# Down projection: the fourth weight sum of each block is made by an accumulating DMA instead of VectorE

## The reference

```python
h = jnp.einsum('btd,df->btf', x, ffn_w_up)
h, new_ffn = causal_dwconv(ffn_hist, h, ffn_conv_w, ffn_conv_b)
hu, hg = jnp.split(h, 2, axis=-1)
f = jnp.einsum('btf,fd->btd', jax.nn.silu(hg) * hu, ffn_w_down)
x = layer_norm(ALPHA * x + f, ln2_g, ln2_b)
```

## Time and profile before

| | us |
|---|---|
| time, median of 3 runs (2047.17 to 2049.23) | 2048.83 |
| the profiled execution | 2046.75 |
| its span in the trace | 2044.9 |
| PE busy | 1992.1 (97%) |
| DVE busy | 1664.3 (81%) |
| ACT busy | 990.7 (48%) |
| POOL busy | 396.7 (19%) |

### The profile page before, as it was taken

One profiled execution on the slowest core, in us unless ns is written; L12 is line 12 of the kernel. 1 busy time (PEld: TensorE's weight loads), 2 busy tenths in 40 slices (PEclk: granted clock), 3 DMA queues, 4 the chain that ended last, 5 costly groups with the idle time before them and its releaser, 6 DMA issues. The chain is left out here.

```text
span 2044.9 us, 42398 instructions
## 1 busy us (share of the span) xinstructions
PE 1992.1 (97%) x15639; PEld 1972.5 (96%) x15639; DVE 1664.3 (81%) x2623; ACT 990.7 (48%) x1503; POOL 396.7 (19%) x552
## 2 busy tenths in 40 slices
PE   9999999999996999999999999999999999999995
PEld 8999999999996999999999999999999999999995
DVE  3698899987699877777777777777778889899898
ACT  4445444433565444444444444444446545454445
POOL 0022222120640211111111111111111121112212
PEclk9999999999997999999999999999999999999998
DMA  6322222123656766767667677676666898779973
GB/s 223 99 78 78 82 88 71 55 83 125 205 155 204 203 176 185 190 176 189 185 180 196 175 184 192 176 193 175 184 189 205 219 242 213 207 196 233 220 177 121
DMA packets 123246, 344.00 MB, mean 168 GB/s; under 512 B 14404, under 2 KB 24900, under 8 KB 123136
## 3 DMA queue, kind: packets, MB, share of 16 engines
q1 hardware_dynamic: 94336, 260.40, 38.0%
q0 software_dynamic: 27792, 80.19, 22.9%
q10 hardware_dynamic: 1008, 1.93, 0.3%
HBM read 314.04 MB, written 23.97 MB: 165 GB/s over the span
## 5 line engine op out<-in xcount | busy, mean ns | idle before, releaser
L1017 PE MATMUL acc<-comb,w_hi 128*128 128x274 f32 x4784 | 921.2, 292 | 17.6 <-DVE comb L2171 12.7
L1017 PEld LDWEIGHTS acc<-comb,w_hi 128*128 128x128 f32 x4784 | 759.6, 190 | 19.4 <-DVE comb L2171 7.4
L1017 PE MATMUL acc<-comb,w_lo 128*128 128x274 f32 x2392 | 693.0, 290 | 0.0
L1017 PEld LDWEIGHTS acc<-comb,w_lo 128*128 128x128 f32 x2392 | 458.0, 191 | 0.0
L1132 PE MATMUL acc<-comb,w_hi 128*128 128x272 f32 x2240 | 424.4, 288 | 3.6 <-DVE w_lo L2309 3.0
L1132 PEld LDWEIGHTS acc<-comb,w_hi 128*128 128x128 f32 x2240 | 352.3, 189 | 5.9 <-DVE w_lo L2309 3.6
L1132 PE MATMUL acc<-comb,w_lo 128*128 128x272 f32 x1120 | 323.3, 289 | 0.0
L1422 ACT ACTIVATE w_hi<-sum 128x1024 fp32r<-128x1024 f32 x172 | 182.4, 1060 | 239.9 <-PE acc L1017 137.2
L2119 DVE TENSOR_TENSOR w_lo<-sum,w_hi 128x1024 fp32r<-128x1024 f32 x172 | 210.8, 1226 | 81.0 <-ACT w_hi L1422 76.3
L2119 DVE TENSOR_TENSOR w_lo<-raw_a,w_hi 128x1024 fp32r<-128x1024 f32 x125 | 152.9, 1223 | 101.1 <-ACT w_hi L1422 101.1
L1132 PEld LDWEIGHTS acc<-comb,w_lo 128*128 128x128 f32 x1120 | 210.8, 188 | 0.0
(11 more groups left out here) (301 smaller groups left out, 3155.5 us busy)
## 6 DMA issues: line engine op xcount, KB each, us to landing
raw_a<-w_up SPq DMA_DIRECT2D x127, 512.0 KB, 6.1
stage<-w_stream SPq DMA_DIRECT2D x90, 512.0 KB, 3.3
sum<-w_up POOLq DMA_DIRECT2D x89, 512.0 KB, 7.0
sum<-w_up SPq DMA_DIRECT2D x88, 512.0 KB, 3.3
d_a<-w_down SPq DMA_DIRECT2D x96, 320.0 KB, 4.8
act_spill<-prod_f SPq DMA_DIRECT2D x43, 272.0 KB, 5.7
d_s<-w_down SPq DMA_DIRECT2D x32, 320.0 KB, 4.8
d_s<-w_down POOLq DMA_DIRECT2D x32, 320.0 KB, 6.5
```

The source lines that it names most:

```text
L1017: mm = pe.matmul(bank(b), wt[:, k * P:(k + 1) * P], prod_comb(j, k, c), start=start and q == 0, stop=stop and q == 2, skip_group_check=True)
```

## The change

The fourth sum is no longer an instruction of DVE. POOL issues an accumulating DMA (`sum_d_s4`) that adds quarter 1 of the block's weights, read again from HBM, to `d_s2`. It stands in POOL's stream after `add_x1` and before the sums of block b+2. It waits for the low part of product 2 (`up_lo`) and for its forerunner (`s4_first`, a semaphore that the up stage had used once, hence the 16). ACT's rounding for product 5 waits for its landing in place of `s4_made`. SP's load of `d_a12` of block b+1 no longer waits for the sum, only for the low part of product 1.

```diff
@@ SP
                 if b + 1 < N_BLOCKS:
-                    sp.wait_ge(s4_made, FT + b)
                     sp.wait_ge(up_lo, nth_down(b, 1))
                     load_d_a12(b + 1)
@@ ACT, down_top
                 elif s == 5:
-                    act.wait_ge(s4_made, FT + b)
+                    act.wait_ge(s4_first, 16 + 16 * (b + 1))
                     weight_top(n, d_s2[:, :])
@@ DVE
-            def make_d_s4(b):
-
-                dve.wait_ge(a12_in, 16 * (FT + b))
-                dve.wait_ge(up_lo, nth_down(b, 2))
-                dve.tensor_tensor(d_s2[:, :], d_s2[:, :], d_a12[:, :], ALU.add).then_inc(s4_made, 1)
...
                     low_after(b, s)
-                    if s == 1:
-                        make_d_s4(b)
@@ POOL
+            def sum_d_s4(b):
+
+                pool.wait_ge(up_lo, nth_down(b, 2))
+                pool.wait_ge(s4_first, 16 + 16 * b)
+                pool.dma_start(d_s2[:, :], dram["w_down"][b * 4 + 1], accum_op=ALU.add).then_inc(s4_first, 16)
...
                 if 1 <= b <= 8:
                     add_x1(b - 1)
+                sum_d_s4(b)
                 if b + 2 < N_BLOCKS:
                     sum_d_s1(b + 2)
```

## The result

| | before | after |
|---|---|---|
| median, us (lowest to highest) | 2048.84 (2047.17 to 2049.23), 4 runs | 2130.78 (2128.17 to 2131.39), 4 runs |
| ratio, with 95% interval | | 1.0406 (1.0394 to 1.0418) |
| profiled execution, its span | 2046.75, 2044.9 | 2130.52, 2128.9 |

The change costs 82 us. The direction was forecast, the size was not: 2081 was named, with a range up to 2112.

The account below looks back on a forecast made before the run. PE bounds the kernel, busy 97% of the span. Losses of 16.0, 14.4, 3.2 and 2 less 1 gained make 34.6 us, 32 after 3 off; 2046.75 becomes 2078.75, plus 2.08 to the median 2081, range 2062 to 2112.

Parts of the forecast that it names:

- the chain behind it: Before product 5: rounding 0.74, low part 0.73, add 0.44 and some 0.2 for hand-overs, 2.1 us together.
- a landing by 7.4: Block 13: the fourth sum must land by 7.4 us into the block, 1.4 after ACT's start in the kernel before.
- healing: Blocks 1 to 8: a stall before product 5 moves the next add_x1 and deadline back, so the 4.7 us loss partly shrinks.
- No healing: Rival, chance 0.11: each of 16 blocks loses its full 4.7 or 4.9 us, 77 us, with the rest 2130.
- the term 8 x 2.0 + 8 x 1.8: Loss of 2.0 us a block in blocks 1 to 8 (16.0) and 1.8 in blocks 18 to 25 (14.4).
- the round of the chain: Blocks 1 to 8: one d_s1 sum's issue to the next, 13.22 us, 15.2 with the new DMA, against a 13.2 block.
- the floors that I had for these two: Least landing of add_x1 with nothing in front (2.3 plus 3.3 us), and the new DMA's own work behind it, 1.96 us.
- my lower bound: Blocks 1 to 8: even with nothing ahead of add_x1, the new DMA lands 1.3 us after its deadline.
- the floor of 21 us: DMA engines at 94.8% plus 15% make 110%, so 16 blocks take at least 1.3 us more each, 21 us.
- the 3 us taken off: Deduction for SP's earlier d_a12 load, said to shorten the round a little: 34.6 becomes 32 us.

Follow-up runs that it names:

- The filler: Changed kernel plus 14 matmuls of ones (3.29 us) on PE ahead of product 5 in blocks 1 to 8 and 17 to 23: 2123.32 us, ratio 1.0377.
- The same traffic with the wait: Kernel before plus a 480-column accumulating DMA into an unused tile, whose landing ACT awaits before rounding for product 5: 2104.75 us, ratio 1.0273.

## Why the prediction was right and wrong

**Right: what is gained.** I took 1 us for VectorE's 26 us; leaving the sum out altogether gave 1.2, with an interval from 3.7 gained to 0.2 lost. The reading was that PE is busy 13.20 of 13.20 us and waits three times.

**Right: the place and the chain.** The waits are before product 5, ACT stands before the landing, and the chain behind it was worked out as 2.1 us and took 2.09. In block 6 product 5 could have started at about 1711.6, so ACT's latest start was 1709.5, 7.6 us into the block; I had a landing by 7.4. In the quiet blocks the DMA lands 4.7 us after issue in the median, mostly in time, and blocks 9 to 16 lost 2.2 us in all, with three waits of up to 0.5.

**Right: healing.** `add_x1` landed 6.5 us after issue where it took 9.1 before; in the run with the extra DMA, where nothing waits, it still takes 9.2 in the median, so it is the stalls that give the queue time. `add_shift` did not land sooner after its issue (11.6 us in the median where it was 10.3); what heals in blocks 18 to 25 is that it is issued 2.5 to 5.6 us before the block begins, where it was between 2.8 before and 0.9 behind. "No healing" named 2130 and the time is 2130.78, but its mechanism is refuted: the late part of the landing did shrink. That the number fits is chance, a smaller wait with a clock cost on top.

**Wrong: the term 8 x 2.0 + 8 x 1.8.** Measured idle time is 23.5 us in blocks 1 to 8 (2.9 a block) and 19.5 in blocks 18 to 25 (2.4 a block), with block 0 at 3.0 instead of 1.6. In the sum it is 51.8 against 34.6. The step that failed is "Between 1.3 and 4.7 I take the round of the chain", with its "With 1.96 more in this chain it is 15.2, against a block of 13.2: 2.0 us a block". That chain, from one `d_s1` sum to the next, doesn't close the loop: POOL stood idle in it for 9.11 us, waiting for a load. The loop that closes goes through PE: last product of a block, issue of `add_x1`, its landing, the fourth sum's landing, rounding and low part, product 5, product 6, and so again the last product. Of it the landing of the fourth sum was 2.7 us behind that of `add_x1`, not 1.96. With the numbers after: 1.0 to the issue of `add_x1`, 6.5 to its landing, 2.7 to the fourth sum's, 0.1 until ACT starts, 2.1 for the chain, and 2 x 1.886 for the products: 16.2 us at full clock. All but the 6.5 and the 2.7 could be read before, and with the floors that I had for these two (5.6 and 1.96) the loop gives 14.6, which is my lower bound again. So I had this loop, as a bound, and took the value from a chain with slack in it. For blocks 18 to 25 the loop isn't worked out. Their waits are uneven, from 0.6 us (blocks 23 and 24) to 5.7 (block 25), and why is open.

**Wrong: a term is missing.** The sum has nothing for the products behind a wait. PE's granted clock falls in most of the blocks with a long one: 15.7 us more busy time in blocks 1 to 8, 10.4 in 18 to 25, 3.0 in block 0. The page has 32.2; the other 3.1 are spread (1.0 of them in blocks 9 to 16, where the clock is 1.00, so not all of it is clock). Products 5 and 6 come right after the wait, so they are in the loop: 16.2 and 15.7 / 8 = 2.0 are 18.2, against a measured block of 147.0 / 8 = 18.4. The filler shows how much is its own: 8.8 of the 39.2 us that blocks 1 to 8 lost came back, about 10 without the filler's overrun, not 15.7. The reading is that a slow product also gives the queue time. So of a busy time that has grown, only a part comes back.

**Wrong: the floor of 21 us, and the 3 us taken off.** 103% of the engines cost nothing. Of 110%, that I had worked out from shares before, nothing is to be seen: after, queue 0 and queue 1 hold 54.3 + 28.9 = 83.2% in the same 60 us of the span, in blocks that have become longer. For the 3 us of the earlier `d_a12` load no run stands alone; nothing shows them.

The account: forecast 32; to it 17.2 of waits (51.8 - 34.6), 32.2 of busy time, and the 2.6 taken off (34.6 - 32), 84.0. Of these about 2.5 lie ahead of the stage, which begins at 1593.9 instead of 1591.4; in the profiles of the other kernels it begins at 1590.2 to 1593.8, so this part need not come from the change.

**Still open.** Why the fourth sum lands 2.7 us after `add_x1` and not 1.96. The loads of queue 1 may have a part in it, as it was 1.7 with them held back, but that is one kernel, and there the queue ahead was another. It also grows with the size: block by block, the median is 1.6 for 160 KB, 2.0 for 240 KB and 2.7 for 320 KB. Open too is which waits cost clock.

No version beats the kernel before. The two at its level are the one that leaves the sum out and the one in which VectorE makes it and nothing waits for the DMA.

## What to carry to other kernels

When a sum is moved from a hidden engine to a DMA, ask for its deadline and for what stands ahead of it in its queue, and close the loop through the engine that sets the pace, with the biggest transfer in it; a landing whose median only just meets the deadline already loses (27.5 us here with 5.2 against 5.4). Busy shares of DMA engines, even above 100%, say nothing about whether one transfer lands in time. A wait of TensorE for some microseconds can bring slower products behind it, which want a term of their own, and here taking that price away gave only a part of it back.

## What was not expected of the hardware

- The shares of two DMA queues add up to 103% for 60 us without any loss, so a share is time that packets took, not a capacity used.
- After a wait of 3.74 us the granted clock of product 5 was 0.57, and the product took 3.35 us instead of 1.886. After the wait of 1.54 us in block 17 it stayed at 1.00. The length alone doesn't tell: 1.77 us (block 19) was followed by 0.58, and 3.23 us in block 19 of "The same traffic with the wait" by 1.00.
- 3.29 us of matmuls with ones in the wait kept the clock at 1.00 in eight blocks.
- An accumulating DMA of 320 KB landed in no less than 4.2 us (4.3 for the fourth sum after the change) and a plain copy in 3.0, through the same queue.
